# A two-block transformer kernel: the position key copied for one head and spread by GpSimd, other slots for the head norms, and the output projections opened chunk by chunk

## The reference

```
h = rms_norm_2(x, norm1_g[l])
z = h @ w_in[l]
(cq, ckv, kpe, gq, gk, gv, glr, gr, su, gates) = split_in(z)
...
o_a = mla_mixer(cq, ckv, kpe, ...)      # 8 heads, 64 + 32 wide, head norms, rope, softmax
o_b = gla_mixer(gq, gk, gv, glr, gr, ...)
o_c = s5_mixer(su, ...)                 # a scan over complex states
...
x = x + merged @ w_out[l]
h2 = rms_norm_2(x, norm2_g[l])
x = x + jnp.square(jax.nn.relu(h2 @ w_ff1[l])) @ w_ff2[l]
```

## Time and profile before

| | |
|---|---|
| median of three runs | 2382.57 us (2380.13 to 2386.01) |
| the profiled execution's own time | 2379.96 us |
| its span | 2377.9 us |
| TensorE busy | 2205.1 us, 93% |
| VectorE busy | 1785.8 us, 75% |
| ScalarE busy | 1350.4 us, 57% |
| GpSimd busy | 277.1 us, 12% |
| granted TensorE clock, mean | 0.975 |

### The profile page before, as it was taken

One profiled execution on the slowest core, in us unless ns is written; L12 is line 12 of the kernel. 1 busy time (PEld: TensorE's weight loads), 2 busy tenths in 40 slices (PEclk: granted clock), 3 DMA queues, 4 the chain that ended last, 5 costly groups with the idle time before them and its releaser, 6 DMA issues.

```text
span 2377.9 us, 42135 instructions
## 1 busy us (share of the span) xinstructions
PE 2205.1 (93%) x17214; PEld 2064.8 (87%) x17214; DVE 1785.8 (75%) x3196; ACT 1350.4 (57%) x2113; POOL 277.1 (12%) x308
## 2 busy tenths in 40 slices
PE   2989999999999999999999898898999998898999
PEld 2978899989998898998998885788999875788999
DVE  5898778678759887775778788976668788876653
ACT  3578886466446888854664536454553535444542
POOL 0000000022000000000221332300004232200000
PEclk9999999999989999999999999999999999898999
DMA  7545466567755464664665423244655313243554
GB/s 279 181 164 179 160 204 223 182 199 231 237 169 173 153 201 153 206 221 144 190 202 169 128 62 111 89 155 139 195 183 189 126 54 118 89 160 133 186 189 132
DMA packets 110849, 395.72 MB, mean 166 GB/s; under 512 B 12320, under 2 KB 13888, under 8 KB 110400
## 3 DMA queue, kind: packets, MB, share of 16 engines
q1 hardware_dynamic: 96768, 343.52, 44.3%
q0 software_dynamic: 12160, 44.08, 5.7%
q10 hardware_dynamic: 1728, 5.43, 0.6%
HBM read 391.93 MB, written 1.05 MB: 165 GB/s over the span
## 4 chain that ended last, share of the span: by engine, by line
PE 70%; DVE 17%; ACT 8%; issue 3%; DMA 1%; SPq 0%; DVEq 0%; ACTq 0%
PE bank L534 69%; DVE WL L1403 4%; ACT scr L966 3%; ACT WH L966 2%; ACT L955 2%; DVE arena L1467 2%; DMA ring<-in_w 1%; DVE arena L2022 1%; DVE arena L1581 1%; DVE scr L1656 1%; ACT arena L966 1%; DVE scr L1580 1%; DVE scr L1643 0%; DVE scr L1450 0%; DVE small L1655 0%
## 5 line engine op out<-in xcount | busy, mean ns | idle before, releaser
L966 ACT ACTIVATE WH<-ring 128x1024 fp32r<-128x1024 f32 (+1 forms) x638 | 671.1, 1053 | 856.5 <-PE bank L534 828.5
L534 PE MATMUL bank<-HTH,WH 128*128 128x256 f32 x3392 | 978.1, 288 | 39.9 <-DVE HTL L1443 12.3
L534 PE MATMUL bank<-HTL,WH 128*128 128x256 f32 x3392 | 963.9, 284 | 0.0
L534 PE MATMUL bank<-HTH,WL 128*128 128x256 f32 x3392 | 962.7, 284 | 0.0
L1403 DVE TENSOR_TENSOR WL<-ring,WH 128x1024 fp32r<-128x1024 f32 (+2 forms) x616 | 748.4, 1225 | 150.3 <-ACT WH L966 149.0
L534 PEld LDWEIGHTS bank<-HTH,WH 128*128 128x128 f32 x3392 | 651.3, 192 | 61.1 <-issue 48.6
L534 PEld LDWEIGHTS bank<-HTL,WH 128*128 128x128 f32 x3392 | 651.3, 192 | 1.7 <-issue 1.4
L534 PEld LDWEIGHTS bank<-HTH,WL 128*128 128x128 f32 x3392 | 650.7, 192 | 0.0
L955 ACT ACT_TABLE_LOAD x110 | 141.1, 1283 | 22.6 <-DMA arena<-in_crow 13.9
L534 PE MATMUL bank<-ff2h,WH 128*128 128x256 f32 x512 | 144.0, 281 | 0.0
L534 PE MATMUL bank<-ff2l,WH 128*128 128x256 f32 x512 | 143.8, 281 | 0.0
(11 more groups left out here) (284 smaller groups left out, 3850.5 us busy)
## 6 DMA issues: line engine op xcount, KB each, us to landing
ring<-in_w SPq DMA_DIRECT2D x620, 512.0 KB, 4.2
arena<-in_wada POOLq DMA_DIRECT2D x80, 512.0 KB, 4.7
ring<-in_w SPq DMA_DIRECT2D x16, 384.0 KB, 3.5
arena<-in_wada SPq DMA_DIRECT2D x8, 512.0 KB, 19.7
arena<-in_wada ACTq DMA_DIRECT2D x8, 512.0 KB, 22.1
ring<-in_w SPq DMA_DIRECT2D x8, 288.0 KB, 2.8
arena<-in_s POOLq DMA_DIRECT2D x4, 512.0 KB, 5.1
cst<-in_cst SPq DMA_DIRECT2D x1, 1025.0 KB, 6.6
```

Of the source, the lines that this page charges most:

```text
L534: ins = e.matmul(out, a, b, start=(start and i == 0), stop=(stop and i == len(pairs) - 1))
L966: return e.activation(out, a, func, **kw)
```

## The change

The position key is copied by VectorE for one head only; GpSimd copies it to the other seven, between its turns for q = 5 and q = 6, and `heads` waits for that copy. The slots of `heads0`, `heads1` and `cutm` change. In stages 0, 2, 4 and 6 the first three units of `res` are run by `opening`, whose activations are now looked up. VectorE forms both `lo` of the two later units one slot ahead of such an opening, as it does at the start of a stage.

```
+        self.opens = set(self.base[:8]) | {g.units[0].i for g in self.groups
+                                           if g.kind == "res" and g.gi == 0 and g.stage in (0, 2, 4, 6)}
...
-    "heads0": [29, 30, 32, 34, 35, 37, 39, 40, 42, 44, 45, 47, 49, 50],
...
+    "heads0": [30, 31, 34, 35, 36, 39, 40, 42, 43, 44, 46, 48, 49, 50],
...
             def opening(xs):
 
+                hi, lo = SOURCE[xs[0].src]
...
-                        mm(o, [(wh[:, k, :], HTH[:, k, :]), (wh[:, k, :], HTL[:, k, :])], start=(k == 0 and x.first),
+                        mm(o, [(wh[:, k, :], hi[:, k, :]), (wh[:, k, :], lo[:, k, :])], start=(k == 0 and x.first),
                            stop=False)
-                        ins = mm(o, [(wl[:, k, :], HTH[:, k, :])], start=False,
+                        ins = mm(o, [(wl[:, k, :], hi[:, k, :])], start=False,
...
-                if u in plan.base:
+                if u in plan.opens:
                     opening(units[u:u + 3])
-                elif u - 1 not in plan.base and u - 2 not in plan.base:
+                elif u - 1 not in plan.opens and u - 2 not in plan.opens:
...
-                    ready = [ev_scalar("q2", l, bi, st), ev_scalar("k2", l, bi, st), ev_vector("pe", l, 0, st)]
+                    ready = [ev_scalar("q2", l, bi, st), ev_scalar("k2", l, bi, st), LB.G("pe", l)]
...
-                    e.tensor_copy(KH[64:96, :, :], ps[64:96, 0:T].unsqueeze(1).to_broadcast([32, 8, T])).then_inc(
-                        ev_vector.inc(k, l, gi, st), 1)
+                    e.tensor_copy(KH[64:96, 0, :], ps[64:96, 0:T]).then_inc(ev_vector.inc(k, l, gi, st), 1)
...
-                for v in (() if u in plan.base else (u + 2, u + 3) if u + 1 in plan.base else (u + 2,)):
+                for v in (() if u in plan.opens else (u + 2, u + 3) if u + 1 in plan.opens else (u + 2,)):
...
-                        turns(l, range(2, 8))
+                        turns(l, range(2, 6))
+                        p.wait_ge(LC.G("ct", l, 5), ev_vector("pe", l, 0, 4 + 2 * l))
+                        e.tensor_copy(KH[64:96, 1:8, :], KH[64:96, 0, :].unsqueeze(1).to_broadcast(
+                            [32, 7, T])).then_inc(LB.G.inc("pe", l), 1)
+                        p.wait_ge(LB.G("pe", l))
+                        turns(l, range(6, 8))
```

More of the change, by code:

```diff
@@ L322 @@
     "norms": [8, 9, 10, 11],
-    "heads0": [29, 30, 32, 34, 35, 37, 39, 40, 42, 44, 45, 47, 49, 50],
-    "heads1": [30, 31, 33, 35, 36, 38, 40, 41, 43, 45, 46, 48, 50, 51],
-    "cutm": [53],
+    "heads0": [30, 31, 34, 35, 36, 39, 40, 42, 43, 44, 46, 48, 49, 50],
+    "heads1": [32, 33, 36, 37, 38, 41, 42, 44, 45, 46, 48, 50, 51, 52],
+    "cutm": [55],
     "s5": turn_ticks(6, 32, 8, 5) + [57, 58, 59, 60, 61],
```

## The result

The changed kernel takes 2390.27 us (median of 20 runs, 2385.13 to 2398.66), the kernel before 2385.12 us (20 runs, 2380.0 to 2389.19). The ratio is 1.0027 with a 95% interval of 1.0016 to 1.0037: 5.2 us slower by the medians and 6.4 by the ratio. That is clear of the noise, and still under the 0.3% (7 us) that the prediction had set as its edge. The profiled execution took 2385.13 us (span 2383.0), 5.2 more than that of before; both are near the fastest of their kernel. In what follows "before" and "after" are these two profiled executions; layer 0 stands for both layers unless layer 1 is named.

What follows compares the result with a forecast made beforehand. TensorE was taken as the bound (works 93% of the span). Per layer 6.0 - 1.75 - 0.9 = +3.35 us, two layers +6.7, stage a 0: 2386.7 us, 2389 against the runs' median; range 2376 to 2403.

Steps and rivals of the forecast that it cites:

- its own case: Whole kernel: heads cost 4 to 9 us a layer, total +3 to +13 us; chance 0.38.
- The chain to the wait: Squares of `heads0` wait for GpSimd's copy behind the turns for q = 5; TensorE stands still 12.3 us.
- The rival of the dear copy: At `heads0`: copy takes 4.3 us, turns 10.1, wait kept in full; +19 us, 2402 us; chance 0.19.
- The half clock behind the wait: At the sum of squares after TensorE's wait: half clock adds 1.0 us.
- Given back: Behind 1500 us, new slots thin VectorE's work: 2.2 of 9 us a layer come back.
- The heads: `heads0` and `heads1`, wait less what returns: cost 6.0 us a layer, between -1 and 12.2.
- Until 1500 us VectorE is full, so spacing can't help there: Heads' stretch before 1500 us: VectorE busy 19.83 of 20 us, so the new slots gain nothing there.
- the waits of 4.1 and 3.1 us would be shorter: TensorE's waits on VectorE past 1500 us: shorter with the new slots.
- the faster rival: Waits past 1500 us and half clock go, openings reach their best: -10.5 us, 2372 us; chance 0.14.
- The key's copy: VectorE's copy falls to 0.3 to 0.4 us; TensorE's wait for its bank ends, -1.75 us a layer, bound 0.
- The openings: `res`: stage c wait falls from 3.28 to 2.4 us, -0.9 a layer; stage a gives 0.
- with the half clock avoided at best -2.5: `res` of stage c: the openings' best gain is 2.5 us a layer if half clock is avoided too.

Runs made afterwards that it cites:

- Late against early: Changed kernel, with GpSimd's key copy behind the turns for q = 5 (ratio 1.0027), against the same with the copy ahead of them (0.9945).
- new slots alone: Kernel before with the new slots of `heads0`, `heads1` and `cutm` and nothing else: 2381.35 us, ratio 0.9981.
- early copy: Changed kernel, but GpSimd copies the position key ahead of the turns for q = 5, not behind them: 2372.76 us, ratio 0.9945 to the kernel before.

## Why the prediction was right, and what in it was not

It forecast 6.7 us more; 5.2 were measured, so its own case came in. The chain that makes the wait was right. Two terms of the sum were too small in size, a cost and a gain, and they offset each other: that the total is so near is partly luck.

- **The chain to the wait held.** GpSimd's turns took 8.8 us, as forecast; the copy 1.67 us (1.6); TensorE stood still 12.8 us (12.3); the gain of `heads0` came at 1462.20 (1462.1). The last figure hides two errors: the turns began 1.0 us earlier than I had it (1443.95, not 1445.0), and the sum of squares took 1.8 us more than 1.96, not 1.0. A copy that reads one tensor is priced like a memset of its size. The rival of the dear copy needed 4.3 us.
- **The half clock behind the wait was too small.** I added 1.0 us, for the sum alone; the rows say 2.9 us. The example of the Trainium skill ("TensorE: Matmul & The Clock Gate", HAM oscillation) has 1.67 us throttled, half of which is lost, 0.8 us: short of the 2.9 too.
- **Given back.** I took 2.2 of 9 us. Late against early, the 12.8 us at unit 33 are 11.1 at the next sum of squares, and 9.8 a layer by the ratios. The new slots alone gain 2.3. The heads therefore cost 9.8 - 2.3 = 7.5 us a layer where I had 6.0; with some 2.7 us of uncertainty a layer the two don't part, and both are in the range that I gave. "Until 1500 us VectorE is full, so spacing can't help there" failed: with the new slots alone VectorE waits 4.09 us there. So did the sign that the waits of 4.1 and 3.1 us would be shorter: TensorE waits 4.76 us at 1514.56. (Two small slips: full speed is 0.12 us a matmul in the rows, not 0.11; and the faster rival, with the openings at their best, needed 7.5 us given back, not 8.2.)
- **The key's copy.** 0.42 us, and nobody waits for it, as forecast. Of the 1.75 us a layer some 1.3 came through (with an interval from nothing to 2.7); the bound that I named, 0, is not excluded.
- **The openings, the term that was mis-sized most.** The wait at `res` is 2.25 us (2.4) and stage a gives nothing, both as forecast. But stage c alone, in the kernel before, gave 4.1 us a layer (2.7 to 5.5) where I had 0.9, outside my bound of 2.5. Taken out of the changed kernel, the openings were worth 2.0 a layer (0.1 to 3.9). The step that failed is "with the half clock avoided at best -2.5": it looked at `res` alone and not at the next stage's start, where the clock is worth 1.8 us a layer.
- **The sum.** 7.5 - 1.3 - 4.1 = 2.1 us a layer, 4.2 in all, against 5.2 measured and 6.7 forecast. The heads' cost was too small by 1.5 a layer and the openings' gain by 3.2; the total hid both. With the openings at the 2.0 of the changed kernel the sum is 8.4. Both are within what the ratios can tell (3.8 to 8.8 us).
- **The rule of the Trainium skill against the copy** ("SBUF — State Buffer", SBUF: two separate sides) would have it take its time from VectorE. In the changed kernel VectorE waits then. The other way round the rows agree in direction: turns and copy are slower beside a busy VectorE, 11.2 and 2.55 us where they took 8.8 and 1.67 beside an idle one. With the early copy they agree from VectorE's side: two scans, which read two tensors each, take 3.11 us beside it and 1.68 without it.

## What to carry to other kernels

A helper's work goes into its queue by the time at which its input is there and its result is wanted, not at the end of a group that it has nothing to do with: here one instruction twelve places earlier was worth 20 us. The best place is one where the other engines' work doesn't slow it, nor it theirs: the early copy still cost VectorE 1.4 us a layer. When a stall can't be avoided, moving its consumer back doesn't simply shorten it, since the work that fills the gap may slow the producer. A removed wait on TensorE is worth its length and the half clock behind it, which isn't to be read from the wait's length; here it was also worth half clock behind the next short wait, in code that wasn't touched; so compare the granted clock for some 50 us behind each change, over several executions.

## What the hardware did that I had not expected

- The half clock (1.2 GHz) behind a stall of TensorE doesn't follow the stall's length. At the same sum of squares it lost nothing behind 3.01 us, 6.0 us behind 2.87, 5.1 behind 7.29, 2.6 behind 8.9, 2.9 behind 12.8 and 5.5 behind 14.5.
- Behind one and the same wait of 2.75 us at a stage boundary the granted clock over 8 us was 0.63, 0.8 or 1.00, a spread of 3 us. A comparison of single executions at one place is worth no more than that: in layer 0 the untouched stage d was 2.6 us faster after (187.9 us against 190.5), and the clock of its first 8 us, 1.00 against 0.63, is worth 3.0.
- A copy of 32x1792 on GpSimd took 1.67, 1.96 or 2.55 us, with what VectorE did beside it; and beside the copy of 1.95 us VectorE's two scans took 3.11 us instead of 1.68.
